# 32x32-block transposes on VectorE, with reordered expert weight rows, in place of three TensorE transposes per expert block

## The chip, the cores and the metric

The kernel runs on one core of one Trainium2 chip, in fp32. The metric is device time in microseconds (us), the median of several executions. In profiles PE is TensorE (PEld its weight loads), DVE is VectorE, ACT is ScalarE, POOL is GpSimd, and SP is SyncE, whose queue issues nearly all DMA transfers. PSUM is the tensor `ps`, eight banks of 128 x 512 fp32. TensorE's clock has two levels, 1.2 and 2.4 GHz; the profile gives the granted share of the higher one.

## The reference, cut to what matters

512 tokens of width 1024 go through two layers. Layer 0 mixes tokens by retention, layer 1 by a Conformer convolution. Each mixer is followed by a mixture of 32 experts in 4 groups, of which every token takes the best group and the best two experts inside it:

```python
h = rmsnorm(x, norm_ffn_g[i])
lg = xt @ w_rg + b_rg                       # group scores, top 1
le_sel = (xt @ w_re + b_re)[group]          # expert scores in the group, top 2
for each block of tokens that share an expert e:
    y = (silu(xblk @ w_gate[e]) * (xblk @ w_up[e])) @ w_down[e]
x = x + sum of the weighted y of each token
```

`w_gate[e]` and `w_up[e]` are 1024 x 512 and `w_down[e]` is 512 x 1024, all fp32: 6 MB for one expert, 192 MB for a layer. The kernel uses every expert in each layer.

## The kernel before, in words

The program is hand-scheduled: each engine runs its own list of instructions, and semaphores order them. The change lies in the expert stage, which occurs twice (layers `l` = 0 and 1).

**The weights.** An expert's weights come in three DMA transfers of 2 MB: `w_gu0` (gate and up, first half of the 1024 rows), `w_gu1` (second half) and `w_down`. There are nine places of 2 MB, three experts deep: `slots_of = [(0, 1, 2), (3, 4, 5), (6, 7, 8)]`. Places 0 to 5 lie in `ring`, 6 in `area_c`, 7 in `area_b` and 8 in `hT`; the profile names them so. The first three experts of a layer are loaded before its expert stage begins. SP then issues the three loads of expert e+3, in order, each once the last block of expert e has used the place: `gu_half` after the first half product, `gu_mm` after the second, `y_mm` after the down product (line 304 issues them). All go to one queue.

**The blocks.** An expert's tokens are cut into blocks of 32, at least one for each expert; the number is known only at run time, and loops with register bounds (`one_block`, `experts`) run over them. The profiled execution runs 46 blocks in layer 0 and 48 in layer 1. TensorE does for block t:

1. `gu` half 0 (L770): 16 products of the block's 32 rows, held transposed in `hgT`, with `w_gu0`, four column groups side by side.
2. `put_rows(0)` (L753): 16 products that scatter the block before, split in `y_hi` and `y_lo`, to the first 256 tokens by `slot_tok`, a 0/1 matrix. The result lies in banks 4 to 7.
3. `gu` half 1 (L770). Gate is then in `ps[:, 2, 0:128]` and up behind it, with 32 rows in each group of 32 partitions.
4. `pick_rows(t+1)` (L700): 16 products gather the next block's rows from `xn` by a 0/1 matrix, to `ps[:, 0, 0:256]`.
5. The transpose of `a_e`, the block's activation (L782).
6. `put_rows(1)` (L753): the other 256 tokens, again in banks 4 to 7. It waits until VectorE has added the first half to `x` (`added`).
7. `turn_block(t+1)` (L709): two transposes of `hg`, the next block's rows.
8. The down product `y` (L790) with `aT_e` and `w_down`.

VectorE adds the scattered tokens to `x` in four pieces (`add_tile`, L1132), computes `a_e` = silu(gate) * up (L1143), copies the picked rows from PSUM to `hg` (`stage`, L1020), multiplies their transpose by the norm gain into `hgT` (`turned_block`, L1008), forms `y_lo` (L1150), and prepares the next 0/1 matrix (`know_rows`, L996 to L1002). ScalarE computes `sg_e` = silu(gate) (L506), copies the transposed activation from PSUM to `aT_e` (L508) and rounds y to `y_hi` (L511). GpSimd builds `slot_tok` (L455).

A matrix row of `hg` holds, in partition 32g+s, columns 256g to 256g+255 of row s. TensorE's full 128 x 128 transposes bring column 256g+128c+p of that to partition p.

Of the kernel before, what the change touches and what calls it, by code (L numbers as in the profile page):

```python
# [21 lines left out]
ALU = mybir.AluOpType  # L22
# [7 lines left out]
P = 128  # L30
# [28 lines left out]
G_MIX, G_FFN, G_HEAD, B_PW1, B_DW, LN_G, LN_B, W_DW = 0, 16, 32, 48, 64, 72, 80, 88  # L59
NPAR = W_DW + KT * WIDTH  # L60

# [31 lines left out]
def program(nc, x_in, pos_in, const_in, decay_in, par_in, w_qk, w_v, w_g, w_out, w_pw1, w_pw2, b_pw2,  # L93
            w_router, b_router, w_gu0, w_gu1, w_down, g_final, tok_in, out):
    with ExitStack() as ctx:
        def sb(name, shape, dt=F32):
            return ctx.enter_context(nc.sbuf_tensor(name, shape, dt))
# [41 lines left out]
        block_rows = sb("block_rows", [P, NT, BLK])  # L139
        hg = sb("hg", [P, QW])  # L140
        hgT = sb("hgT", [P, KT, BLK])
# [116 lines left out]
        def both(name):  # L258
            return sems(name, NL)
# [6 lines left out]
        gu_half = both("gu_half")  # L266
        t1_mm, hgT_ready, gu_mm, silu_ready, act_ready, t2_mm, aT_ready, y_mm = (
            both(n) for n in ("t1_mm", "hgT_ready", "gu_mm", "silu_ready", "act_ready", "t2_mm", "aT_ready", "y_mm"))

# [190 lines left out]
        def _(act):  # L460
# [35 lines left out]
            def expert_blocks(l):  # L496
                act.wait_ge(exp_arg[l], 1)
                nc.scalar.activation(group_exp, group_exp, ACT.Exp).then_inc(exp_ready[l], 1)
                act.wait_ge(exp_arg[l], 2)
                nc.scalar.activation(expert_exp, expert_exp, ACT.Exp).then_inc(exp_ready[l], 1)  # L500
                act.wait_ge(cum_ready[l], 1)
                total = act.value_load(cum[0:1, NE:NE + 1], min_val=NE, max_val=NBLK - 1)
                act.wait_ge(idx_ready[l], 1)
                with act.Fori(0, total) as t:
                    act.wait_ge(gu_mm[l], t + 1)
                    nc.scalar.activation(sg_e[:, :], ps[:, 2, 0:P], ACT.Silu).then_inc(silu_ready[l], 1)  # L506
                    act.wait_ge(t2_mm[l], t + 1)
                    nc.scalar.copy(aT_e[:, :], ps[:, 3, 0:P]).then_inc(aT_ready[l], 1)  # L508
                    act.wait_ge(y_mm[l], t + 1)
                    act.wait_ge(second_mm[l], t + 1)  # L510
                    nc.scalar.activation(y_hi[:, :], ps[:, 3, P:P + QW], ACT.Copy,  # L511
                                         scale=slots[:, bass.ds(t + NBLK, 1)]).then_inc(y_rounded[l], 1)
# [117 lines left out]
        def _(pe):  # L630
# [73 lines left out]

            def turn_block(l, t):

                pe.wait_ge(staged[l], t + 1)
                for c in range(2):
                    last = nc.tensor.transpose(ps[:, 1, c * P:(c + 1) * P], hg[:, c * P:(c + 1) * P], ident)  # L709
                last.then_inc(t1_mm[l], 1)  # L710

            def route(l):
# [25 lines left out]
                pick_rows(l, 0)  # L738
                turn_block(l, 0)
                pe.wait_ge(spread_ready[l], 1)  # L740
# [17 lines left out]
            def one_block(l, t, turn, s_gu0, s_gu1, s_down):  # L758
# [21 lines left out]
                pick_rows(l, t + 1)  # L780
                pe.wait_ge(act_ready[l], t + 1)
                nc.tensor.transpose(ps[:, 3, 0:P], a_e[:, :], ident).then_inc(t2_mm[l], 1)  # L782
                pe.wait_ge(added[l], 4 * t + 6)
                put_rows(1, 4, second_mm[l])
                turn_block(l, t + 1)
                pe.wait_ge(aT_ready[l], t + 1)
# [154 lines left out]
        def _(dve):  # L941
# [61 lines left out]

            def turned_block(l, t, gain):

                dve.wait_ge(t1_mm[l], t + 1)
                for c in range(2):
                    ins = V.tensor_tensor(  # L1008
                        hgT[:, :, :].rearrange("p (q c) s -> p c q s", c=2)[:, c],
                        ps[:, 1, c * P:(c + 1) * P].rearrange("p (q s) -> p q s", q=4),  # L1010
                        par[:, gain:gain + KT].rearrange("p (q c) -> p c q", c=2)[:, c].unsqueeze(2)
                        .to_broadcast([P, 4, BLK]), ALU.mult)
                ins.then_inc(hgT_ready[l], 1)

            def stage(l, t):

                if not (isinstance(t, int) and t == 0):
                    dve.wait_ge(t1_mm[l], t)
                dve.wait_ge(pick_mm[l], t + 1)
                V.tensor_copy(hg[:, :], ps[:, 0, 0:QW]).then_inc(staged[l], 1)  # L1020

            def route(l, gain):
                dve.wait_ge(logitT_mm[l], 1)
# [18 lines left out]
                for i in range(NT):  # L1042
# [65 lines left out]
                                          coef[:, 0, :].unsqueeze(2).to_broadcast([P, 8, NBLK]), ALU.mult))  # L1108
                turned_block(l, 0, gain)
                link.done(V.tensor_tensor(block_hot_r[:, 1], block_hot[:, :, :],  # L1110
# [24 lines left out]

            def expert_blocks(l, gain, n):
                total = dve.value_load(cum[0:1, NE:NE + 1], min_val=NE, max_val=NBLK - 1)
                with dve.Fori(0, total) as t:
                    dve.wait_ge(first_mm[l], t + 1)
                    add_tile(0, 4).then_inc(added[l], 1)  # L1140
                    add_tile(1, 4).then_inc(added[l], 1)
                    dve.wait_ge(silu_ready[l], t + 1)
                    V.tensor_tensor(a_e[:, :], sg_e[:, :], ps[:, 2, P:2 * P], ALU.mult).then_inc(act_ready[l], 1)  # L1143
                    stage(l, t + 1)
                    dve.wait_ge(second_mm[l], t + 1)
                    add_tile(2, 4).then_inc(added[l], 1)
                    turned_block(l, t + 1, gain)
                    add_tile(3, 4).then_inc(added[l], 1)
# [96 lines left out]
            expert_norm(0, 1)  # L1245
            route(0, G_FFN)
            expert_blocks(0, G_FFN, 2)


# [85 lines left out]
            expert_norm(1, 3)  # L1335
            route(1, G_FFN + KT)
            expert_blocks(1, G_FFN + KT, 4)


# [83 lines left out]
```

## Time and profile before

| | us |
|---|---|
| median of 3 executions | 1647.12 (1646.97 to 1655.14) |
| the profiled execution, its own time | 1646.21 |
| span in its trace, first to last instruction | 1644.2 |
| expert loop of layer 0, first `gu` to the end of the last `y` | 473.0 to 922.2 |
| expert loop of layer 1 | 1165.8 to 1628.7 |

The span is cut into 40 slices of 41.1 us in the page's pictures, with a digit for the busy tenths of each. Chain rows, followed back from the last instruction, show what released what; a DMA row in the chain lasts from the issue of a transfer to its landing, with its time in the queue.

### The profile page before, as it was taken

How to read it: one execution, taken by the hardware profiler on the slowest of the kernel's cores; microseconds unless marked ns; L12 is line 12 of the kernel's file. 1: busy time of each engine (PE TensorE's matmuls, PEld its weight loads, DVE VectorE, ACT ScalarE, POOL GpSimd, SP SyncE). 2: the span in 40 equal slices, each digit the busy share in tenths (PEclk: the TensorE clock that was granted, in tenths of full speed). 3: DMA queues.
4: the chain of work that ended last, by engine and by line, in shares of the span. 5: the costliest groups of instructions: out<-in, count | busy, mean ns of one | idle time of the engine just before them, and what ended most of it. 6: DMA issues, size and time to landing. Idle time of an engine off the chain costs nothing.

```text
span 1644.2 us, 45941 instructions
## 1 busy us (share of the span) xinstructions
PE 1547.2 (94%) x19216; PEld 1008.3 (61%) x19217; DVE 967.9 (59%) x1669; ACT 467.8 (28%) x802; POOL 424.9 (26%) x371
## 2 busy tenths in 40 slices
PE   7999999999989999999889899889899999989996
PEld 6868678687645555555455588556555555555553
DVE  4222112220377777777657889943777777767777
ACT  5242422423312222222212432054122222222223
POOL 3434344243101121121112255511011121111211
PEclk9999999999999999999999999999999999999998
DMA  9212122122479999999999421036199999999994
GB/s 372 102 53 101 53 83 81 67 85 97 159 310 427 428 428 429 429 428 428 428 429 428 209 103 52 23 121 266 44 428 427 428 429 428 428 429 428 430 428 186
DMA packets 33849, 457.57 MB, mean 278 GB/s; under 512 B 3840, under 2 KB 3968, under 8 KB 6400
## 3 DMA queue, kind: packets, MB, share of 16 engines
q1 hardware_dynamic: 33648, 456.55, 66.5%
q8 instruction: 46, 0.75, 0.2%
q10 hardware_dynamic: 144, 0.17, 0.0%
q14 instruction: 11, 0.09, 0.0%
HBM read 454.61 MB, written 2.10 MB: 278 GB/s over the span
## 4 chain that ended last, share of the span: by engine, by line
PE 83%; DMA 8%; DVE 4%; issue 2%; ACT 2%; POOL 1%; DVEq 0%; SPq 0%; ACTq 0%; POOLq 0%
PE ps L770 19%; PE ps L658 10%; PE ps L660 10%; PE ps L659 10%; PE ps L790 9%; PE ps L700 9%; PE ps L753 7%; DMA area_b<-w_gu 6%; DMA ring<-w_down 2%; PE ps L858 2%; PE ps L709 2%; PE ps L782 1%; POOL area_c L439 1%; PE ps L908 1%; PE ps L850 1%
## 5 line engine op out<-in xcount | busy, mean ns | idle before, releaser
L1132 DVE TENSOR_TENSOR x<-x,ps 128x1024 f32<-128x1024 f32 x384 | 458.9, 1216 | 132.3 <-PE ps L753 132.3
L455 POOL TENSOR_SCALAR slot_tok<-trig,slot_now 128x512 fp32r<-128x512 f32 x94 | 147.0, 1564 | 719.3 <-PE ps L753 719.3
L424 POOL TENSOR_TENSOR w_lo<-ring,w_hi 128x512 fp32r<-128x512 f32 x176 | 237.8, 1354 | 356.1 <-ACT w_hi L474 356.0
L770 PE MATMUL ps<-ring,hgT 128*32 128x256 f32 x4160 | 255.9, 387 | 24.8 <-issue 21.0
L474 ACT CAST w_hi<-ring 128x512 fp32r<-128x512 f32 x176 | 108.8, 622 | 345.2 <-PE ps L660 345.2
L770 PEld LDWEIGHTS ps<-ring,hgT 128*32 128x32 f32 x4160 | 127.7, 111 | 122.0 <-issue 41.9
L700 PE MATMUL ps<-area_a,block_rows 128*32 128x256 f32 x3072 | 184.1, 380 | 2.6 <-DVE block_rows L1000 2.6
L700 PEld LDWEIGHTS ps<-area_a,block_rows 128*32 128x32 f32 x3072 | 100.4, 110 | 70.1 <-issue 5.3
L506 ACT ACT_TABLE_LOAD x94 | 120.6, 1283 | 33.2 <-DVEq L1122 31.5
L658 PE MATMUL ps<-w_hi,hT_hi 128*128 128x512 f32 x320 | 125.0, 391 | 2.9 <-DVE hT_lo L1322 2.9
L790 PE MATMUL ps<-ring,aT_e 128*32 128x256 f32 x2080 | 125.7, 382 | 0.2 <-DMA ring<-w_down 0.2
L659 PE MATMUL ps<-w_lo,hT_hi 128*128 128x512 f32 x320 | 124.6, 389 | 0.0
L660 PE MATMUL ps<-w_hi,hT_lo 128*128 128x512 f32 x320 | 124.5, 389 | 0.0
L753 PE MATMUL ps<-y_hi,slot_tok 32*128 32x256 f32 x1536 | 120.8, 329 | 2.8 <-DVE y_lo L1150 2.8
L511 ACT ACTIVATE y_hi<-ps,slots 128x256 fp32r<-128x256 f32 x94 | 44.6, 475 | 261.2 <-PE ps L790 261.2
L753 PEld LDWEIGHTS ps<-y_hi,slot_tok 32*128 32x128 f32 x1536 | 74.4, 184 | 55.3 <-issue 40.1
L506 ACT ACTIVATE sg_e<-ps 128x128 f32<-128x128 f32 x94 | 26.1, 278 | 274.1 <-PE ps L770 274.1
L658 PE MATMUL ps<-hT_hi,w_hi 128*128 128x512 f32 x256 | 99.8, 390 | 3.2 <-DVEq L1171 2.5
L753 PE MATMUL ps<-y_lo,slot_tok 32*128 32x256 f32 x1536 | 100.5, 276 | 0.0
L1020 DVE COPY hg<-ps 128x256 f32<-128x256 f32 x96 | 40.8, 425 | 100.4 <-PE ps L700 100.4
L659 PE MATMUL ps<-hT_lo,w_hi 128*128 128x512 f32 x256 | 99.6, 389 | 0.0
L660 PE MATMUL ps<-hT_hi,w_lo 128*128 128x512 f32 x256 | 99.6, 389 | 0.0
(217 smaller groups left out, 2067.4 us busy)
## 6 DMA issues: line engine op xcount, KB each, us to landing
ring<-w_gu SPq DMA_DIRECT2D x88, 2048.0 KB, 21.0
ring<-w_down SPq DMA_DIRECT2D x44, 2048.0 KB, 22.6
area_c<-w_gu SPq DMA_DIRECT2D x20, 2048.0 KB, 23.4
area_b<-w_gu SPq DMA_DIRECT2D x20, 2048.0 KB, 25.9
hT<-w_down SPq DMA_DIRECT2D x20, 2048.0 KB, 25.9
ring<-w_pw SPq DMA_DIRECT2D x6, 2048.0 KB, 11.1
ring<-w_qk SPq DMA_DIRECT2D x4, 2048.0 KB, 9.5
ring<-w_v SPq DMA_DIRECT2D x4, 2048.0 KB, 8.8
```

Source lines behind the costliest of these rows:

```text
L424: nc.gpsimd.tensor_tensor(w_lo[:, place, :], ring[:, s, at:at + 512], w_hi[:, place, :].bitcast(F32), ALU.subtract).then_inc(lo_ready, 1)
L455: nc.gpsimd.tensor_scalar(slot_tok[:, :], tok_number, slot_now[:, 0:1], None, ALU.is_equal).then_inc(tok_hot[l], 1)
L474: nc.scalar.copy(w_hi[:, place, :], ring[:, s, at:at + 512]).then_inc(hi_ready, 1)
L506: nc.scalar.activation(sg_e[:, :], ps[:, 2, 0:P], ACT.Silu).then_inc(silu_ready[l], 1)
L658: nc.tensor.matmul(at, lhs[0], rhs[0], start=start, stop=False)
L659: nc.tensor.matmul(at, lhs[0], rhs[1], start=False, stop=False)
L660: return nc.tensor.matmul(at, lhs[1], rhs[0], start=False, stop=stop)
L700: last = nc.tensor.matmul(ps[32 * g:32 * g + 32, 0, 0:QW], block_rows[:, i, :], xn[:, i, g * QW:(g + 1) * QW], start=(i == 0), stop=(i == ...
L753: last = nc.tensor.matmul(ps[:, bank + g, i * QW:(i + 1) * QW], slot_tok[rows, cols], part[rows, :], start=(i == 0 and n == 0), stop=(i == ...
L770: last = nc.tensor.matmul(ps[32 * g:32 * g + 32, 2, 0:256], hgT[:, n * (KT // 2) + k, :], gate_up[n][:, k, :, g * P:(g + 1) * P], start=(n ...
L790: last = nc.tensor.matmul(ps[32 * g:32 * g + 32, 3, P:P + QW], aT_e[:, k * BLK:(k + 1) * BLK], down[:, k, g * 256:(g + 1) * 256], start=(k ...
L1132: return V.tensor_tensor(x[:, i, :].rearrange("p (g c) -> p g c", g=4), x[:, i, :].rearrange("p (g c) -> p g c", g=4), ps[:, bank:bank + 4 ...
```

## The change

`hg` is made by VectorE's `transpose`, which transposes each 32 x 32 block by itself, straight from PSUM; `turned_block` then multiplies it by the gain, from SBUF to SBUF, in one instruction. `aT_e` is made by VectorE from `a_e` in the same way. TensorE's transposes of `hg` and `a_e` go, and so does ScalarE's copy to `aT_e`. After a blockwise transpose the partition 32g+j holds row 256g+32k+j of the model dimension in piece k, instead of row 128k+p. So the host lays the rows of all expert weights out in this order (`tiled`; the transfers have the same size and form), and the gains, 16 more columns of `par`, are laid out in it too (`strips`).

```diff
-        t1_mm, hgT_ready, gu_mm, silu_ready, act_ready, t2_mm, aT_ready, y_mm = (...)
+        hgT_ready, gu_mm, silu_ready, act_ready, aT_ready, y_mm = (...)
...
 # ScalarE, one block
                     nc.scalar.activation(sg_e[:, :], ps[:, 2, 0:P], ACT.Silu).then_inc(silu_ready[l], 1)
-                    act.wait_ge(t2_mm[l], t + 1)
-                    nc.scalar.copy(aT_e[:, :], ps[:, 3, 0:P]).then_inc(aT_ready[l], 1)
                     act.wait_ge(y_mm[l], t + 1)
...
 # TensorE
-            def turn_block(l, t):
-
-                pe.wait_ge(staged[l], t + 1)
-                for c in range(2):
-                    last = nc.tensor.transpose(ps[:, 1, c * P:(c + 1) * P], hg[:, c * P:(c + 1) * P], ident)
-                last.then_inc(t1_mm[l], 1)
...
                 pick_rows(l, t + 1)
-                pe.wait_ge(act_ready[l], t + 1)
-                nc.tensor.transpose(ps[:, 3, 0:P], a_e[:, :], ident).then_inc(t2_mm[l], 1)
                 pe.wait_ge(added[l], 4 * t + 6)
                 put_rows(1, 4, second_mm[l])
-                turn_block(l, t + 1)
                 pe.wait_ge(aT_ready[l], t + 1)
...
 # VectorE
             def stage(l, t):
 
                 if not (isinstance(t, int) and t == 0):
-                    dve.wait_ge(t1_mm[l], t)
+                    dve.wait_ge(hgT_ready[l], t)
                 dve.wait_ge(pick_mm[l], t + 1)
-                V.tensor_copy(hg[:, :], ps[:, 0, 0:QW]).then_inc(staged[l], 1)
+                V.transpose(hg[:, :, :].rearrange("p k s -> p (k s)"), ps[:, 0, 0:QW]).then_inc(staged[l], 1)
+
+            def turned_block(l, t):
+
+                dve.wait_ge(staged[l], t + 1)
+                V.tensor_tensor(hgT[:, :, :], hg[:, :, :],
+                                par[:, G_ROWS + KT * l:G_ROWS + KT * (l + 1)].unsqueeze(2).to_broadcast([P, KT, BLK]),
+                                ALU.mult).then_inc(hgT_ready[l], 1)
...
                     V.tensor_tensor(a_e[:, :], sg_e[:, :], ps[:, 2, P:2 * P], ALU.mult).then_inc(act_ready[l], 1)
+                    dve.wait_ge(act_ready[l], t + 1)
+                    V.transpose(aT_e[:, :], a_e[:, :]).then_inc(aT_ready[l], 1)
                     stage(l, t + 1)
+                    turned_block(l, t + 1)
                     dve.wait_ge(second_mm[l], t + 1)
                     add_tile(2, 4).then_inc(added[l], 1)
-                    turned_block(l, t + 1, gain)
                     add_tile(3, 4).then_inc(added[l], 1)
...
 # host
     def tiled(w):
 
         rows, cols = w.shape[2:]
-        return w.reshape(NL, NG, NPG, rows // P, P, cols).transpose(0, 2, 1, 4, 3, 5).reshape(NL, NE, P, SLOT)
+        return w.reshape(NL, NG, NPG, 4, rows // P, BLK, cols).transpose(0, 2, 1, 3, 5, 4, 6).reshape(NL, NE, P, SLOT)
```

The block of the loop as TensorE has it, from the second half product on. Before:

```order
L770 MATMUL ps<-ring,hgT 32x256 x16
L695 REGISTER_ALU
L700 MATMUL ps<-area_a,block_rows 32x256 x16
L782 MATMUL ps<-const,a_e 128x128
L783 REGISTER_ALU
L753 MATMUL ps<-y_hi,slot_tok 128x256 x4
L753 MATMUL ps<-y_lo,slot_tok 128x256 x4
L753 MATMUL ps<-y_hi,slot_tok 128x256 x4
L753 MATMUL ps<-y_lo,slot_tok 128x256 x4
L709 MATMUL ps<-const,hg 128x128 x2
L790 MATMUL ps<-ring,aT_e 32x256 x16
```

The same place on TensorE in the changed kernel:

```order
L761 MATMUL ps<-ring,hgT 32x256 x16
L694 REGISTER_ALU
L699 MATMUL ps<-area_a,block_rows 32x256 x16
L772 REGISTER_ALU
L744 MATMUL ps<-y_hi,slot_tok 128x256 x4
L744 MATMUL ps<-y_lo,slot_tok 128x256 x4
L744 MATMUL ps<-y_hi,slot_tok 128x256 x4
L744 MATMUL ps<-y_lo,slot_tok 128x256 x4
L778 MATMUL ps<-ring,aT_e 32x256 x16
```

The three transposes are gone, and nothing else on TensorE has moved. VectorE's block before, from its first two additions to `y_lo`:

```order
L1132 TENSOR_TENSOR x<-x,ps 128x1024 x2
L1143 TENSOR_TENSOR a_e<-sg_e,ps 128x128
L1019 REGISTER_ALU
L1020 COPY hg<-ps 128x256
L1132 TENSOR_TENSOR x<-x,ps 128x1024
L1008 TENSOR_TENSOR hgT<-ps,par 128x4x32 x2
L1132 TENSOR_TENSOR x<-x,ps 128x1024
L1150 ISA
L1150 SCALAR_TENSOR_TENSOR y_lo<-ps,slots,y_hi 128x256
```

The same place on VectorE in the changed kernel:

```order
L1116 TENSOR_TENSOR x<-x,ps 128x1024 x2
L1127 TENSOR_TENSOR a_e<-sg_e,ps 128x128
L1129 STREAM_TRANSPOSE aT_e<-a_e 128x128
L996 REGISTER_ALU
L997 STREAM_TRANSPOSE hg<-ps 128x256
L1002 TENSOR_TENSOR hgT<-hg,par 128x256
L1116 TENSOR_TENSOR x<-x,ps 128x1024 x2
L1136 ISA
L1136 SCALAR_TENSOR_TENSOR y_lo<-ps,slots,y_hi 128x256
```

The copy to `hg` has become a transpose, one more transpose stands ahead of it, and the multiplication into `hgT`, once in two parts between the last two additions, stands ahead of both.

## Rows read from the trace of the kernel before

**Rows 1.** The page's picture of the span, 40 slices: granted clock, DMA.
```profile
PEclk9999999999999999999999999999999999999998
DMA  9212122122479999999999421036199999999994
```

**Rows 2.** The page's DMA issues: form, count, KB, median us to landing.
```profile
ring<-w_gu SPq DMA_DIRECT2D x88, 2048.0 KB, 21.0
```

**Rows 3.** Windows of the expert stages: busy us by engine, PEclk, DMA share, GB/s.
```profile
790.00:840.00 50.00, 40.53 (x656) 22.42 (x648) 27.63 (x49) 9.21 (x16) 6.99 (x8) 0.93 1.01 428
1240.00:1290.00 50.00, 49.00 (x866) 28.29 (x862) 36.48 (x64) 11.78 (x21) 10.12 (x11) 1.00 1.01 429
1440.00:1490.00 50.00, 45.47 (x771) 26.07 (x767) 32.36 (x58) 11.23 (x19) 8.74 (x10) 0.97 1.01 429
```

**Rows 4.** The chain that ended last, one block: start us, us, what.
```profile
1572.22 1.75 PE ps L770 x32
1573.97 0.67 PE ps L753 x14
1574.64 1.86 PE ps L770 x32
1576.51 1.73 PE ps L700 x32
1578.23 0.26 PE ps L782
1578.49 0.68 PE ps L753 x15
1579.17 0.37 PE ps L709 x2
1579.54 1.86 PE ps L790 x32
```

**Rows 5.** The same chain: transfers in it, from issue to landing.
```profile
856.39 35.67 DMA ring<-w_down
...
1379.94 27.63 DMA area_b<-w_gu
...
1418.86 32.76 DMA area_b<-w_gu
```

**Rows 6.** SP's transfers: first expert loads of each layer's loop, and the last.
```profile
476.86 3.09 SPq L304 DMA_DIRECT2D ring<-w_gu  x2
...
1188.36 2.71 SPq L304 DMA_DIRECT2D ring<-w_gu  x2
...
1599.78 0.33 SPq L304 DMA_DIRECT2D ring<-w_down  x1
```

**Rows 7.** The chain again: the last down product of each layer.
```profile
920.30 1.91 PE ps L790 x32
...
1626.78 1.91 PE ps L790 x32
```

**Rows 8.** Timeline, VectorE and the down product in one block; idle before in brackets.
```profile
612.12 0.28 DVE L1143 TENSOR_TENSOR a_e<-sg_e,ps 128x128 f32<-128x128 f32 x1
613.45 0.42 DVE L1020 COPY hg<-ps 128x256 f32<-128x256 f32 x1 [1.05 <-PE ps L700]
...
614.37 1.22 DVE L1132 TENSOR_TENSOR x<-x,ps 128x1024 f32<-128x1024 f32 x1 [0.49 <-PE ps L753]
...
614.62 1.93 PE L790 MATMUL ps<-ring,aT_e 128*32 128x256 f32 x32
615.50 0.48 DVE L1008 TENSOR_TENSOR hgT<-ps,par 128x128 f32<-128x128 f32 x2
...
617.34 0.48 DVE L1150 SCALAR_TENSOR_TENSOR y_lo<-ps,slots,y_hi 128x256 fp32r<-128x256 f32 x1 [0.23 <-ACT y_hi L511]
```

**Rows 9.** The page's costliest groups: GpSimd's, busy, mean ns, idle before.
```profile
L455 POOL TENSOR_SCALAR slot_tok<-trig,slot_now 128x512 fp32r<-128x512 f32 x94 | 147.0, 1564 | 719.3 <-PE ps L753 719.3
```

**Rows 10.** Timeline, TensorE: a half product after a wait for its weights.
```profile
1446.78 3.60 PE L770 MATMUL ps<-area_c,hgT 128*32 128x256 f32 x32 [2.87 <-DMA area_c<-w_gu]
```

More of the change, by code:

```diff
@@ L59 @@
 G_MIX, G_FFN, G_HEAD, B_PW1, B_DW, LN_G, LN_B, W_DW = 0, 16, 32, 48, 64, 72, 80, 88
-NPAR = W_DW + KT * WIDTH
+G_ROWS = W_DW + KT * WIDTH
+NPAR = G_ROWS + NL * KT
 DEPTH = 3
@@ L139, in program @@
         block_rows = sb("block_rows", [P, NT, BLK])
-        hg = sb("hg", [P, QW])
+        hg = sb("hg", [P, KT, BLK])
         hgT = sb("hgT", [P, KT, BLK])
@@ L266, in program @@
         gu_half = both("gu_half")
-        t1_mm, hgT_ready, gu_mm, silu_ready, act_ready, t2_mm, aT_ready, y_mm = (
-            both(n) for n in ("t1_mm", "hgT_ready", "gu_mm", "silu_ready", "act_ready", "t2_mm", "aT_ready", "y_mm"))
+        hgT_ready, gu_mm, silu_ready, act_ready, aT_ready, y_mm = (
+            both(n) for n in ("hgT_ready", "gu_mm", "silu_ready", "act_ready", "aT_ready", "y_mm"))
         after_ret = [64, 64, 64, 64, 0, 0, 0, 0, 0]
@@ L738, in route @@
                 pick_rows(l, 0)
-                turn_block(l, 0)
                 pe.wait_ge(spread_ready[l], 1)
@@ L1002, in know_rows, with route @@
                 V.tensor_scalar(pos[:, :], pos[:, :], -float(BLK), None, ALU.add).then_inc(hot_step[l], 1)
[L1004 to L1013, printed above, removed]
             def stage(l, t):
                 if not (isinstance(t, int) and t == 0):
-                    dve.wait_ge(t1_mm[l], t)
+                    dve.wait_ge(hgT_ready[l], t)
                 dve.wait_ge(pick_mm[l], t + 1)
-                V.tensor_copy(hg[:, :], ps[:, 0, 0:QW]).then_inc(staged[l], 1)
-            def route(l, gain):
+                V.transpose(hg[:, :, :].rearrange("p k s -> p (k s)"), ps[:, 0, 0:QW]).then_inc(staged[l], 1)
[4 more added lines that the diff above has]
+                                ALU.mult).then_inc(hgT_ready[l], 1)
+            def route(l):
                 dve.wait_ge(logitT_mm[l], 1)
@@ L1108, in route @@
                                           coef[:, 0, :].unsqueeze(2).to_broadcast([P, 8, NBLK]), ALU.mult))
-                turned_block(l, 0, gain)
+                turned_block(l, 0)
                 link.done(V.tensor_tensor(block_hot_r[:, 1], block_hot[:, :, :],
@@ L1134, in add_tile, with expert_blocks @@
                                        ps[:, bank:bank + 4, i % 2 * QW:(i % 2 + 1) * QW], ALU.add)
-            def expert_blocks(l, gain, n):
+            def expert_blocks(l, n):
                 total = dve.value_load(cum[0:1, NE:NE + 1], min_val=NE, max_val=NBLK - 1)
@@ L1245, in _ @@
             expert_norm(0, 1)
-            route(0, G_FFN)
-            expert_blocks(0, G_FFN, 2)
+            route(0)
+            expert_blocks(0, 2)
             norm_lo(2, 1, G_MIX + KT)
@@ L1335, in _ @@
             expert_norm(1, 3)
-            route(1, G_FFN + KT)
-            expert_blocks(1, G_FFN + KT, 4)
+            route(1)
+            expert_blocks(1, 4)
 _NAMES = ("x_in", "pos_in", "const_in", "decay_in", "par_in", "w_qk", "w_v", "w_g", "w_out", "w_pw1", "w_pw2", "b_pw2",
@@ L1373, with strips @@
     const, decay = shape_constants()
+    def strips(w):
+        return w.reshape(NL, 4, KT, BLK).transpose(1, 3, 0, 2).reshape(P, NL * KT)
     def columns(w):
@@ L1385 @@
                           columns(a["conv_b_pw1"]), columns(crossed(a["conv_b_dw"])),
-                          columns(crossed(a["conv_ln_g"])), columns(crossed(a["conv_ln_b"])), taps], axis=1)
+                          columns(crossed(a["conv_ln_g"])), columns(crossed(a["conv_ln_b"])), taps,
+                          strips(a["norm_ffn_g"])], axis=1)
     w_in = a["ret_w_in"][0]
```

## The prediction, made before the changed kernel was run

> **What bounds the kernel now.** I began with the picture of the span. In its two long stretches where the DMA digit is 9, slices 12 to 22 and 29 to 39, the expert loops run [rows 1]. The windows there show both candidates for the bound at once: TensorE busy 49.0 of 50 us, and the DMA engines at a share of 1.01 with 428 GB/s [rows 3]. VectorE has 36.5 us of 50. So neither busy share decides; the question is which of the two is late at which point.
>
> The chain of waits answers it. Nearly all of it is TensorE, but at three places it passes through a transfer of 28 to 36 us [rows 5]. A transfer of 2 MB [rows 2] does not take so long: two landings in the same place `area_b`, at 1379.94 + 27.63 = 1407.57 and at 1418.86 + 32.76 = 1451.62, lie 44.05 us apart, and nine transfers (three experts) lie between them, so one takes 4.894 us, which is 2 MB at 428 GB/s. The rest of the 33 us is queue. The weights are a stream without gaps: 87 transfers in each layer, 426 us, from the release of the first place [rows 6] on. Where TensorE catches up with it, it waits: the windows from 790 and from 1440 us show 40.5 and 45.5 us busy of 50 instead of 49 [rows 3].
>
> So a faster block is worth nothing while the stream leads, and only what TensorE does after its last wait for weights can become shorter. Two such stretches exist.
>
> Layer 0: the last wait ends with the landing at 856.39 + 35.67 = 892.06 [rows 5]. Behind it stand the rest of that block and three whole blocks, up to the y at 920.30 [rows 7].
>
> Layer 1: the last wait ends at 1451.62 [rows 5]; from there to the y at 1626.78 [rows 7] TensorE runs 18 whole blocks. The last `w_down` is 34 transfers behind that landing: 1451.62 + 34 x 4.894 = 1618.0. Its y starts at 1626.78, so TensorE is 8.8 us behind the stream at the end. That lag is what the change can collect.
>
> **What a block loses.** One block of the chain is 1.75 + 0.67 + 1.86 + 1.73 + 0.26 + 0.68 + 0.37 + 1.86 = 9.18 us [rows 4]. The transpose of `a_e` (0.26) and the two of `hg` (0.37) go: 0.63 us. The neighbours that now meet (picked rows to `put_rows`, `put_rows` to y) meet elsewhere in the block already in the other order of the same shapes, the half product before `put_rows` at 1.75 and the one behind it at 1.86, so I add nothing for the seams.
>
> **What VectorE gains and loses.** It gets one more instruction of 128 elements, its copy from PSUM of 256 elements becomes a transpose, and the gain becomes one multiplication of 256 instead of two of 128 (0.48 together) [rows 8]. No transpose on VectorE is in the trace. From below I take the same shapes: 0.28 for 128 elements (`a_e`), 0.42 for the copy [rows 8]. From above I take the slowest rate of any row near it, GpSimd's 1.564 us for 512 elements [rows 9], 3.05 ns each: 0.39 and 0.78. I take the lower values, since a copy from the same bank by the same engine is the nearest row. The Trainium skill, VectorE: DVE Perf Modes, section The three transpose paths, gives 311 ns for a 128 x 128 bf16 transpose on VectorE; no run here shows it yet. With that price for `aT_e` and the same 30 ns more on `hg` the sum would come out the same, because both are covered as follows.
>
> `aT_e`: `a_e` ends at 612.40; VectorE then waited until 613.45 for the picked rows (1.05 idle) [rows 8]. The new transpose fits there even at 0.39 or 1.0 us. If that cover were gone, y would wait for it. `put_rows(1)`, which used to stand behind the transpose, now follows the picked rows at once; the additions that it waits for were done when `a_e` started, at 612.12, a microsecond earlier.
>
> `hg` and `hgT`: the transpose runs 613.45 to 613.87, the multiplication to about 614.3. The scatter now ends 0.26 earlier than the 614.37 at which the third addition started [rows 8], so the additions start at 614.3, bound by VectorE, and end near 616.65 without the multiplication between them. y starts at 613.99 instead of 614.62 [rows 8], `y_hi` follows, and `y_lo` may start 2.72 behind y as before, at 616.71. So VectorE has 0.06 us to spare there (it had 0.23 idle [rows 8]) and, after `know_rows`, about half a microsecond before the next additions. It is the engine that is late next. Of a costlier transpose of `hg`, between 0.1 and 0.5 us are free, and all beyond lengthens the block one for one.
>
> ScalarE loses a copy of 0.27 us, on which y depended; it only waits longer. 64 bytes more of `par` per partition and the new order of the weight rows change no transfer's size or form: 0. In front of each loop the first block's two transposes go, under VectorE's work on the block lists: 0.
>
> **The sum, with d = 0.63 saved in each block.** Layer 0: the landing at 892.06 stays, because the first place is released in the very first block [rows 6]. Three whole blocks behind it: 3d = 1.9 us. All other blocks of the layer (46 x 0.63 = 29 us in all) turn into waits for weights.
>
> Layer 1: the first place is released in its third block [rows 6], so the whole stream moves forward by 2d = 1.3 us. Without another wait the 18 blocks would give 18d + 2d = 12.6 us. But TensorE then catches the stream again. The tightest point is expert 28 (three blocks; experts 29 to 31 have one each, as the times of SP's transfers tell). Its `w_down` lies nine transfers before the last, 1618.0 - 44.0 = 1574.0, and is used at 1579.54 [rows 4]: 5.5 us of lag. Thirteen of the 18 blocks end there or before, and 13d = 8.2 is more, so TensorE waits. From there five blocks follow, up to the last y. So the gain is 5.5 + 2d + 5d = 9.9 us. With both layers it is the smaller of 23d and 5.5 + 10d, which cross at d = 0.42: 11.8 us here. Everything behind either loop keeps its length: the conv stage's own weights were already landed or queued, and the tail of layer 1 (additions, norm, output) has no transfer of weights in it.
>
> From this I take off a quarter of one slow half product in each layer, 2 x 0.25 x 1.67 = 0.8 us: after a wait for weights the clock can fall to its lower level, as in the half product of 3.60 us instead of 1.93 [rows 10], and the new waits, for the second halves of the gate and up weights of experts 30 and 28, stand right ahead of the two stretches. That leaves 11.0. The profiled execution took 1646.2 us, 0.9 under the median of the three runs; 1646.2 - 11.0 = 1635.2, and as a median 1636.1 us.
>
> **The rivals.**
>
> *The clock falls in the stretches that count* (0.10). For it: waits of 2 to 3 us are followed by a half product at 1.2 GHz in the trace [rows 10], and such waits become many. Against: most of what is slow then stands ahead of a landing and is hidden. Three slow half products behind the last waits cost 3 x 1.67 = 5.0: a gain of 6.8, 1640.3 us. The Trainium skill says the same of idle stretches (TensorE: Matmul & The Clock Gate, Part 1: activity releases the throttle, idleness lets it return); this trace agrees with its 3.60 us.
>
> *The transposes are slower than copies* (0.10). At 3.05 ns an element `hg` costs 0.36 more; d is then 0.38 to 0.63, the gain 8.7 to 11.8. At 1.0 us for `hg`, d is 0.15 to 0.5 and the gain 3.5 to 10.5: up to 1643 us.
>
> *VectorE becomes the bound and the kernel slower* (0.07). This needs the transpose of `hg` above 1.2 to 1.6 us. At four times the copy, 1.7, a block takes up to 0.5 us more than before, 94 x 0.5 = 47, less some 12 us that the waits for weights of today absorb (8.5 and 3.5 by rows 3): about 1680 us. Nothing in the trace has such a rate on VectorE; only that the instruction is unseen speaks for it.
>
> *Nothing comes of it, since the stream bounds the whole stage* (0.05). For it: the share of 1.01 everywhere. Against: the 8.8 us of lag at the end. It would leave 0 to 2 us: 1646 us.
>
> **Chances and range.** My own case has 0.68, with 1634 to 1638.5 us. A measurement tells about 0.5% (8.2 us) from no change; the gain passes that for d above 0.36. Faster by more than that: 0.68, and 0.05 from the first two rivals, 0.73. Within: 0.20. Slower: 0.07. The range, 1632.5 to 1642, takes in the clock's and the slower transpose's cases, and a gain of 14 if the lag before expert 28 is larger than reckoned.
>
> **What would show it.** In the trace after: blocks of 8.5 us where no weights are awaited; no TensorE row for the transposes; VectorE rows of about 0.3 and 0.43 us for its own; `y_lo` waiting for ScalarE by under 0.1 us or not at all; far more waits for `w_gu` in the middle of both loops; the last landing of layer 0 unchanged against the loop's start and that of layer 1 1.3 us nearer; loops shorter by 1.9 and 9.9 us. A block much over 8.6 us without a wait for weights refutes the VectorE part; a longer spacing than 4.89 us between landings refutes the stream part.

## The result, and the profile after

| | before | after |
|---|---|---|
| median, run side by side | 1647.36 us (6 runs) | 1636.38 us (6 runs, 1635.53 to 1638.92) |
| ratio, 95% interval | | 0.9927 (0.9913 to 0.9942) |
| span of the profiled execution | 1644.2 us | 1633.7 us |
| expert loop of layer 0, first `gu` to the start of the last `y` | 447.2 us | 446.1 us |
| expert loop of layer 1 | 460.9 us | 451.0 us |

The changed kernel is 11.0 us faster by the medians (12.0 by the ratio, 9.6 to 14.3 by its interval); the forecast was 1636.1 us. The picture of its span, from the page (granted clock, DMA), keeps its two stretches of nines in the DMA row. The granted clock has one more 8, in the middle, and its mean over the span is 0.976 instead of 0.986:

```profile
PEclk9999999999999999999899999999999999999998
DMA  9212112122379999999999620026299999999996
```

The same windows as [rows 3]: start and end, length, busy us of PE, PEld, DVE, ACT and POOL, then clock, DMA share and GB/s:

```profile
790.00:840.00 50.00, 37.21 (x596) 20.02 (x596) 27.22 (x45) 7.86 (x11) 6.99 (x8) 0.90 1.01 429
1240.00:1290.00 50.00, 49.00 (x916) 28.28 (x908) 41.05 (x69) 11.88 (x18) 10.47 (x12) 1.00 1.01 428
1440.00:1490.00 50.00, 44.67 (x804) 25.81 (x800) 35.20 (x60) 10.17 (x15) 7.94 (x10) 0.97 1.01 428
```

The DMA engines move what they moved before, 428 GB/s. TensorE, faster by a block's 0.63 us, waits more: 37.2 us busy in the first window instead of 40.5. VectorE's busy time rose from 36.5 to 41.1 us of 50 where no weights are awaited.

One block of the chain that ended last, against [rows 4]:

```profile
1582.51 1.73 PE ps L761 x32
1584.24 0.68 PE ps L744 x16
1584.91 1.86 PE ps L761 x32
1586.78 1.73 PE ps L699 x32
1588.51 0.67 PE ps L744 x15
1589.18 1.86 PE ps L778 x32
```

It sums to 8.53 us instead of 9.18. The rows of 0.26 (L782) and 0.37 (L709) are gone and the others have their old lengths within 0.02. VectorE and the down product in one block, from the timeline, against [rows 8] (idle before in brackets):

```profile
595.06 0.28 DVE L1127 TENSOR_TENSOR a_e<-sg_e,ps 128x128 f32<-128x128 f32 x1
595.37 0.31 DVE L1129 STREAM_TRANSPOSE aT_e<-a_e 128x128 f32<-128x128 f32 x1
596.40 0.45 DVE L997 STREAM_TRANSPOSE hg<-ps 128x256 f32<-128x256 f32 x1 [0.71 <-PE ps L699]
596.88 0.42 DVE L1002 TENSOR_TENSOR hgT<-hg,par 128x256 f32<-128x256 f32 x1
596.93 1.93 PE L778 MATMUL ps<-ring,aT_e 128*32 128x256 f32 x32
597.22 2.34 DVE L1116 TENSOR_TENSOR x<-x,ps 128x1024 f32<-128x1024 f32 x2
599.65 0.48 DVE L1136 SCALAR_TENSOR_TENSOR y_lo<-ps,slots,y_hi 128x256 fp32r<-128x256 f32 x1
```

The transposes take 0.31 and 0.45 us, against 0.42 for the copy that one of them replaces. `aT_e` runs in a hole that was 1.05 us wide and is 0.71 now. `y_lo` has no idle time before it in this block; in the view of waits it had one in all 94 blocks before (21.8 us in all) and has one in 9 now (6.6 us). The Trainium skill (VectorE: DVE Perf Modes, The three transpose paths) gives 311 ns for a 128 x 128 transpose in bf16 on VectorE; the one here is fp32 and took the same 0.31 us.

TensorE's waits for weights in the view of waits (total us, times, longest), for the changed kernel:

```profile
PE ps L761 <- DMA ring<-w_gu: 25.5, 16, 2.3
PE ps L761 <- DMA area_c<-w_gu: 12.0, 5, 2.9
PE ps L761 <- DMA area_b<-w_gu: 8.6, 5, 2.3
PE ps L778 <- DMA ring<-w_down: 3.9, 6, 0.7
PE ps L778 <- DMA hT<-w_down: 1.3, 2, 0.7
PE ps L761 <- issue: 16.4, 18, 1.1
```

For the kernel before, the same view:

```profile
PE ps L770 <- DMA area_c<-w_gu: 5.7, 2, 2.9
PE ps L770 <- DMA area_b<-w_gu: 3.8, 3, 2.3
PE ps L770 <- DMA ring<-w_gu: 3.7, 3, 2.5
PE ps L790 <- DMA ring<-w_down: 0.2, 1, 0.2
PE ps L770 <- issue: 21.0, 23, 1.9
```

The rows with a DMA hold 51.3 us instead of 13.4. So the account of the two loops reads: 94 x 0.63 = 59.2 us taken from TensorE's blocks, of which 37.9 came back as waits for weights. Another 12.0 came back as half products at the lower clock level behind such waits: in the timeline there are 12 of them (2.56 to 3.58 us, together 16.3 over 1.93) instead of 3 (4.3 over). 59.2 - 37.9 - 12.0 = 9.3 us are left, and the two loops are 11.0 us shorter (1.1 and 9.9). The rest consists of smaller terms of both signs, read from the gaps and starts of TensorE's instructions inside the loops. The "issue" gaps ahead of half products, in which TensorE waits for nothing that the profile shows, are 4.4 us shorter (probably since some are now part of a wait for weights). Layer 1's first half product takes 2.75 us instead of 3.64. Against them, the other products, mostly those right behind slow half products, take 3.7 us more. 9.3 + 4.4 + 0.9 - 3.7 = 10.9.

The last wait in each loop, with what follows it, in the chain of the changed kernel (DMA rows last from issue to landing), against [rows 5, 10]:

```profile
850.03 36.74 DMA ring<-w_gu
886.77 0.04 issue
886.81 3.53 PE ps L761 x32
...
1539.15 26.90 DMA ring<-w_gu
1566.05 0.04 issue
1566.09 3.55 PE ps L761 x32
...
1572.11 1.86 PE ps L778 x32
```

Layer 0's last wait still lies three whole blocks ahead of the end, layer 1's moved from 18 blocks ahead to expert 28, five blocks ahead. Both are followed by a half product of 3.5 us, the lower clock level.

SP's first transfers of the loops, against [rows 6]:

```profile
476.68 3.16 SPq L305 DMA_DIRECT2D ring<-w_gu  x2
...
1185.21 2.71 SPq L305 DMA_DIRECT2D ring<-w_gu  x2
```

Layer 1's first place is released 20.04 us into its loop, which starts at 1165.17; before, it was 22.59.

Two single rows answer to [rows 2, 7]. In the page's DMA issues the transfers take 27.9 us to land instead of 21.0: TensorE frees the places sooner, and the queue ahead of them is longer. In the group of the last down product (one tile, one window: count, shortest, median and longest ns, first and last start) layer 1's begins at 1616.2. Its weights landed at 1614.94, 1.26 us earlier; before, they had lain there for 8.7 us.

```profile
ring<-w_gu SPq DMA_DIRECT2D x88, 2048.0 KB, 27.9
```

```profile
L778 PE MATMUL ps<-ring,aT_e x32: 378/379/404, 1616.2 to 1617.8; 128*32 128x256 f32 x32
```

### The profile page after: what moved, and what is told of

It reads as the page before. It is cut to its first block, busy times and chain, and to the rows that moved or that the text cites. A ratio compares the mean times of both kernels' runs of the same rounds, so it can differ in the third digit from the quotient of the medians.

```text
span 1633.7 us, 45273 instructions
## 1 busy us (share of the span) xinstructions
PE 1502.6 (92%) x18930; PEld 982.6 (60%) x18931; DVE 994.7 (61%) x1667; ACT 442.5 (27%) x708; POOL 424.3 (26%) x371
## 4 chain that ended last, share of the span: by engine, by line
PE 67%; DMA 19%; DVE 10%; ACT 2%; issue 1%; POOL 0%; DVEq 0%; SPq 0%; ACTq 0%
PE ps L761 16%; PE ps L657 9%; PE ps L658 9%; PE ps L659 8%; PE ps L778 8%; PE ps L699 7%; DMA area_b<-w_gu 7%; DMA ring<-w_gu 6%; PE ps L744 5%; DMA hT<-w_down 4%; DVE area_c L1278 4%; PE ps L846 2%; DVE ring L1278 2%; DMA ring<-w_down 2%; PE ps L838 1%
## 5 line engine op out<-in xcount | busy, mean ns | idle before, releaser
L1116 DVE TENSOR_TENSOR x<-x,ps 128x1024 f32<-128x1024 f32 x384 | 450.8, 1215 | 100.3 <-PE ps L744 100.3
L761 PE MATMUL ps<-ring,hgT 128*32 128x256 f32 x4160 | 263.2, 396 | 42.1 <-DMA ring<-w_gu 25.5
L778 PEld LDWEIGHTS ps<-ring,aT_e 128*32 128x32 f32 x2080 | 62.3, 109 | 45.4 <-issue 5.2
## 6 DMA issues: line engine op xcount, KB each, us to landing
ring<-w_gu SPq DMA_DIRECT2D x88, 2048.0 KB, 27.9
```

Of the source, the lines that this page charges most:

```text
L761: last = nc.tensor.matmul(ps[32 * g:32 * g + 32, 2, 0:256], hgT[:, n * (KT // 2) + k, :], gate_up[n][:, k, :, g * P:(g + 1) * P], start=(n ...
L778: last = nc.tensor.matmul(ps[32 * g:32 * g + 32, 3, P:P + QW], aT_e[:, k * BLK:(k + 1) * BLK], down[:, k, g * 256:(g + 1) * 256], start=(k ...
L1116: return V.tensor_tensor(x[:, i, :].rearrange("p (g c) -> p g c", g=4), x[:, i, :].rearrange("p (g c) -> p g c", g=4), ps[:, bank:bank + 4 ...
```

## The experiments

Two theories stand against each other throughout. The **stream theory** is the prediction's: the weights' stream sets the pace, and only the blocks behind the last wait for it can shorten a layer. The **proportional rival**: each block is 0.63 us shorter, and a fixed share of it reaches the end everywhere, so that the parts add up. Below, "lag" is the time from the last landing of weights in layer 1 to the start of the `y` that uses them. Each loop and each lag is read from the trace of one execution. Outside the loops executions differ too: the stretch between the loops took 245.5, 246.1 and 250.6 us in three profiled executions (of the kernel before, and of two variants of it below that differ from it only later, in layer 1). So a difference of a few us between two totals says little by itself, and the loops say more.

**Half of the change: block rows only.** `hg` goes by VectorE, `a_e` still by TensorE and ScalarE, and `w_down` keeps its old order of rows. Of the diff above only the lines of `stage`, `turned_block`, `turn_block` and `strips` are made.

```diff
-                turn_block(l, t + 1)
-                V.tensor_copy(hg[:, :], ps[:, 0, 0:QW]).then_inc(staged[l], 1)
+                V.transpose(hg[:, :, :].rearrange("p k s -> p (k s)"), ps[:, 0, 0:QW]).then_inc(staged[l], 1)
```

> Only the block rows are transposed by VectorE; the activation goes through TensorE and ScalarE as before, with w_down in its old row order. d is 0.37 us a block. Theory of the lag (only what TensorE does after its last waits for weights counts; gain the smaller of 23d and 5.5 + 10d): 8.5 us faster than before, up to 1.2 us less for each slow half product right ahead of the last stretches. Rival, every block's saving counts in the same proportion as in the whole change (11.0 us for 0.63): 6.4 us. Rival, VectorE's work has no room: block over 8.85 us.

Measured: 1641.67 us beside 1648.97 for before, ratio 0.9957 (0.9941 to 0.9974), 7.3 us by the medians and 7.1 by the ratio. The block is 8.82 us, 0.37 less, as expected, so VectorE had the room. The time lies between the 8.5 us of the stream theory and the 6.4 of its rival, and by itself decides nothing. Layer 1's loop is 452.8 us and its lag 2.1.

**The other half: activation only.**

```diff
-                    act.wait_ge(t2_mm[l], t + 1)
-                    nc.scalar.copy(aT_e[:, :], ps[:, 3, 0:P]).then_inc(aT_ready[l], 1)
-                pe.wait_ge(act_ready[l], t + 1)
-                nc.tensor.transpose(ps[:, 3, 0:P], a_e[:, :], ident).then_inc(t2_mm[l], 1)
+                    dve.wait_ge(act_ready[l], t + 1)
+                    V.transpose(aT_e[:, :], a_e[:, :]).then_inc(aT_ready[l], 1)
```

> Only the activation is transposed by VectorE, with w_down in the new row order; the block rows go through TensorE as before. d is 0.26 us. Theory of the lag: 6.0 us faster than before, and the gains of this run and of the one with the rows only add up to more (14.5) than the whole change gave (11.0), because alone neither makes TensorE catch the stream again before the last five blocks of layer 1. Rival, gain in proportion to the saving: 4.5 us, and the two add up to 11.0.

Measured: 1642.37 us, ratio 0.996 (0.9946 to 0.9974), so 6.6 us. The block is 8.93, the loop of layer 1 455.9 us, the lag 5.6. By the ratios the two halves sum to 7.1 + 6.6 = 13.7 us, and the whole is worth 12.0 (11.0 by the medians), which leans to the stream theory. The interval of each half is 2.7 us to either side, so this sum alone does not decide. Both halves also had a faster first half product than the changed kernel: in layer 0 it took 2.59 and 2.51 us instead of 3.64, and the last weights landed 432.6 and 432.8 us into the loop, instead of 433.9, which flatters each of them by about 1.2 us. What speaks clearly is the lag of layer 1, 8.7, then 5.6, 2.1 and 1.3 us: it is used up.

**VectorE's room: one transpose more.** The changed kernel with the transpose of `hg` done twice.

```diff
+                for spare in spares:
+                    V.transpose(spare[:, :], ps[:, 0, 0:QW])
```

> The changed kernel with the transpose of the block rows issued once more to a spare tile: VectorE has 0.42 to 0.45 us more in each block, ahead of its last two additions. If VectorE has about 0.4 us of room (by the gap between its y_lo and the next scatter), the block stays within 0.1 us of 8.53 and the time within 1 us of the change's, 10 to 11 us faster than before. If it has only the 0.06 us of the prediction, the block is 8.9 us and the gain 5 to 6 us.

Measured: 1638.65 us, ratio 0.9943 (0.9923 to 0.9964), 10.3 us faster than before by the medians; the block is 8.55, as in the changed kernel (its median there, 8.53 to 8.60). The additional transpose starts 0.37 us before the next one, so it takes 0.37 us of VectorE's time, and the block has room for all of it.

**Three transposes more.** As above, with three places to write to, two of them in `trig`.

> The changed kernel with three more transposes of the block rows to spare tiles, 1.3 us more on VectorE in each block. Theory: room of 0.4, the rest one for one: block 8.53 + 0.95 = 9.5 us, 0.3 us over the kernel before, hence slower than before by about 14 us (the waits for weights of before absorb a part of 94 x 0.3 = 28 us). Rival, VectorE has room for all of it (its busy share is 0.8): no slower than the change. Rival, it had no room at all: block 9.8 us, 30 us slower than before.

Measured: 1643.69 us, ratio 0.9967 (0.9952 to 0.9982). This was expected to lose 14 us to before and gained 5.4: the expectation failed. The timeline shows two reasons.

```profile
595.04 0.45 DVE L1000 STREAM_TRANSPOSE spare<-ps 128x256 f32<-128x256 f32 x1 [0.71 <-PE ps L700]
595.41 0.74 DVE L1000 STREAM_TRANSPOSE trig<-ps 128x256 f32<-128x256 f32 x2
596.07 0.41 DVE L1001 STREAM_TRANSPOSE hg<-ps 128x256 f32<-128x256 f32 x1
596.51 0.43 DVE L1006 TENSOR_TENSOR hgT<-hg,par 128x256 f32<-128x256 f32 x1
596.86 2.35 DVE L1120 TENSOR_TENSOR x<-x,ps 128x1024 f32<-128x1024 f32 x2
...
599.73 0.39 PE L745 MATMUL ps<-y_hi,slot_tok 32*128 32x256 f32 x4 [0.50 <-DVE y_lo L1140]
```

From the first transpose to the additions it takes 1.82 us, against 0.82 in the changed kernel: three transposes add 1.00, not three times 0.45, since each starts before the one ahead of it has ended. And the block is 9.09 us, 0.54 more than 8.55; the last row shows what it waits for, the `y_lo` of the block before. If the block grows one for one past the room, as the prediction has it ("between 0.1 and 0.5 us are free, and all beyond lengthens the block one for one"), VectorE had 1.00 - 0.54 = 0.46 us to spare. The run before this one fits (0.37 cost nothing); the slope itself was not measured, since only this run lies past the room. At 9.09 a block is still shorter than the 9.18 of before, and 19 of the 92 took 8.55 to 8.67 even here, those of layer 1 each right behind a block with a change of expert or a wait for weights. The lag of layer 1 is 3.8 us.

**Half of the stream.** In layer 1 the loads behind the first nine bring only the first half of each place, so that half of the expert weights of 29 experts is left out (old values stand in their stead). This was done to the kernel before and to the changed one. Nothing else differs.

```diff
+                n = SLOT // 2 if l == 1 else SLOT
+                sp.dma_start(places[s][:, 0:n], w[:, 0:n]).then_inc(slot_loaded[s], 16)
```

On the kernel before:

> The kernel before, but in layer 1 every weight load after the first nine moves only the first half of its place (the other half keeps old weights), so the stream of layer 1 needs half the time and TensorE never waits for it. Theory of the lag: TensorE's own pace is left, about 7 us faster than before (the waits for weights in layer 1 go). Rival, TensorE sets the time of the whole stage already: no change.

On the changed kernel:

> The same halved stream in layer 1 under the changed kernel. Theory of the lag: now all 48 blocks of layer 1 count in full, 48 x 0.63 = 30.2 us, and with layer 0's 1 to 2 us this run is 31 to 32 us faster than the one before it with the same halved stream, where the change with the full stream gives 10 to 12. Rival, the 11 us are all that the shorter block is worth: 10 to 12 us here as well.

Measured: 1638.56 us (ratio 0.9931, 0.9907 to 0.9954) and 1606.85 us (0.9733, 0.97 to 0.9767). Both are about as the stream theory had them: 8.9 us faster than before where about 7 were expected, and 31.7 apart where 31 to 32 were. The change is worth 31.7 us once layer 1 moves half the bytes, and 11 when it moves all. Layer 1's loops are 452.3 and 423.7 us; the difference of 28.6 is 48 blocks of 0.60. Windows of the first of the two, then of the second, with the columns of [rows 3]:

```profile
1440.00:1490.00 50.00, 49.05 (x875) 28.46 (x871) 37.03 (x63) 11.78 (x21) 8.73 (x10) 1.00 0.57 204
```

```profile
1440.00:1490.00 50.00, 48.01 (x900) 27.73 (x892) 41.15 (x69) 11.81 (x18) 10.50 (x12) 1.00 0.63 224
```

With the DMA share at 0.57 and 0.63, TensorE is 48 to 49 us busy of 50 in both; VectorE, with one more instruction in a shorter block, reaches 41 us and still holds nothing up. This is the whole value of the change on TensorE. The pair refutes the rival of a fixed share, and VectorE as a bound.

**One transfer more.** An additional 2 MB is moved in layer 1, ahead of the last six loads of weights, to a buffer that nobody reads. If the end hangs on the stream, this costs a transfer's time; where TensorE is late by more than it, nothing.

```diff
+                    if l == 1 and e == LOOPED:
+                        sp.dma_start(aside[:, :], w_gu0[l, e]).then_inc(out_stored, 16)
```

On the kernel before:

> The kernel before with one more transfer of 2 MB (to a buffer in HBM that nobody reads) in the queue ahead of the last six weight loads of layer 1: the last landings come 4.9 us later, or up to twice that as it reads and writes HBM. Theory of the lag: TensorE is 8.7 us behind the last landing, so at 4.9 us the time does not change (0 to 1 us). Rival, the stream sets the time in layer 1: 4.9 us slower.

On the changed kernel:

> The changed kernel with the same additional transfer. Theory of the lag: only 1.3 us of lag are left, so 4.9 us of stream cost 3.6 us and more, against the changed kernel without it (that is 7 to 8.5 us faster than the kernel before instead of 10 to 12). Rival, as much lag as before is left: no cost.

Measured: 1647.55 us (ratio 1.0008, 0.9989 to 1.0028), no cost by the medians, though the interval reaches a cost of 4.6 us; and 1641.61 us (0.997, 0.9952 to 0.9987). That is 5.8 us faster than before by the medians, where 7 to 8.5 were expected, and 5.2 us more than the changed kernel, which was run at another time (7 by the ratios). The traces are clearer. In the kernel before, the lag of 8.7 went down to 4.3 us and the loop stayed at 461.0. In the changed one, the last landing moved by 5.5 us and not 4.9, and the loop by 4.3 us; the lag took the rest. What the totals show beyond 4.3 us, 1 to 3 us, is not explained. The chain of the changed kernel with the transfer ends in a wait:

```profile
1592.29 29.45 DMA ring<-w_down
1621.74 0.14 issue
1621.87 1.97 PE ps L781 x32
```

The last `y` of the program starts 0.13 us after its weights land. In the kernel before, the lag absorbed the transfer; in the changed one nothing does.

**The start of the stream.** With both layers on the stream, its start should count. It hangs on the first half product of a loop, which in the changed kernel stands behind 3.79 us of idle time of TensorE and one short product, and in layer 0 takes 3.64 us instead of 1.93, the lower clock. From the timeline of the changed kernel (the second row is the first half product of layer 0):

```profile
470.66 2.04 PE L733 MATMUL ps<-block_hot_r,slot_hot_r 128*128 128x216 f32 x8 [3.79 <-DVE block_hot_r L1096]
472.84 3.64 PE L761 MATMUL ps<-ring,hgT 128*32 128x256 f32 x32
```

The first attempt put eight idle products there (products of constants whose result nobody reads, to keep TensorE busy), with

```diff
                 pick_rows(l, 0)
+                stay_awake(4, 8)
```

> The changed kernel with eight idle products (128 x 512, 0.46 us each in the trace of the changed kernel) on TensorE behind the first gather of each layer, where it now sits idle for 3.79 us ahead of the product at 470.66 and 1163.24; nothing else differs. In the changed kernel the first half product then takes 3.64 us in layer 0 and 2.75 us in layer 1, instead of 1.93. Theory (the stream of weights sets the end of both layers, and it starts when the first half product releases the first place): the first release comes earlier by 1.7 us in layer 0 and 0.8 us in layer 1, the last landings move by as much, and the kernel becomes 2.5 us faster than the changed one, about 1633.9 us; up to 4 if the product at 470.66 also gets shorter. Rival 1 (the start of the stream decides nothing, the end is set by TensorE's blocks): the two half products save their 2.5 us only if TensorE never waits afterwards, and since it waits in the middle of both loops nothing is left: 1636.4 us. Rival 2 (the clock of the first block doesn't follow from the idle time ahead of it): the first half products stay at 3.6 and 2.8 us, no change, or slower by up to 0.5 us in each layer if the idle products end after the releaser.

Measured: 1639.14 us beside 1649.06 for before, ratio 0.9931 (0.9913 to 0.995): no gain over the changed kernel's 0.9927, where 2.5 us were expected. The half products took 1.93 us and the loops were 444.2 and 449.4 us, shorter by 1.8 and 1.6 than the changed kernel's; but the products took 7.13 us and not 3.7, since one is two rows of the profile, and the loops started 1.9 us later after the gather. The loops became shorter as the theory had it; the filler was mis-sized.

So four products, and the changed kernel once more beside it:

> As the run with eight idle products, but with four. Their time was mis-read there: a row of x8 in the profile is four products (two passes each), so eight took 7.13 us, not 3.7, and ran past the 3.79 us of idle time; the way from the first gather to the loop grew from 6.0 to 7.9 us in each layer, while both loops became shorter (by 1.8 and 1.6 us). Four take 3.68 us and fit. Theory (the stream's start, set by the first release, moves the end of each layer): the loops are as short as with eight (444.2 and 449.4 us, against 446.1 and 451.0 in the changed kernel), and the way to them is 0.4 to 0.6 us shorter than in the changed kernel instead of 1.9 longer; together 4 to 4.5 us faster than the changed kernel run beside it. Rival (the loops were shorter by chance of the clock in their middle): no more than 1 us faster than the changed kernel.

> The changed kernel once more, unchanged, on the chip of the run with four idle products, so that the two are compared there. Both theories: a ratio of 0.9927 to the kernel before, as measured first (0.9913 to 0.9942).

Measured: 1633.31 us (6 runs, 1630.95 to 1638.0), ratio 0.9915 (0.9898 to 0.9932), and 1637.97 us for the changed kernel (6 runs, 1632.28 to 1638.51), ratio 0.9931 (0.9914 to 0.9948). That is 4.7 us between the medians, where 4 to 4.5 were expected and the rival had at most 1. It is not clear of the noise: by the ratios it is 2.6 us, and both the intervals and the ranges overlap. The profile of the kernel with four:

```profile
466.97 3.70 PE L653 MATMUL ps<-const 128*128 128x512 f32 x8
470.83 1.15 PE L734 MATMUL ps<-block_hot_r,slot_hot_r 128*128 128x216 f32 x8 [0.17 <-DVE block_hot_r L1097]
473.00 1.93 PE L762 MATMUL ps<-ring,hgT 128*32 128x256 f32 x32 [1.02 <-issue]
```

The way from the gather to the loop did not get shorter, as I had expected it to (5.97 us in both): what the product at 470.83 gains, an "issue" gap of 1.02 takes. The loops did: 443.5 and 449.2 us, against 446.4 and 451.0 in the changed kernel run beside it, and that is 4.65 us, in one execution of each. The first half products account for 3.64 - 1.93 = 1.7 and 2.68 - 1.93 = 0.8 us of it. Another 1.8 us come from the two slow half products ahead of the stretches that count, which stood in both profiles of the changed kernel and are not there now: in its second one the `y` behind them started 0.97 and 1.07 us after its weights had landed, and now 0.13 in both layers. The chain passes through waits for `w_down` at those places:

```profile
851.84 38.35 DMA ring<-w_down
...
1540.03 27.22 DMA ring<-w_down
1567.25 0.14 issue
1567.38 1.93 PE ps L779 x32
```

The waits ahead of those two half products, from the timelines: 2.10 and 1.99 us in the changed kernel, 2.11 and 2.00 in its second run, all four followed by 3.5 to 3.6 us; 1.13 and 1.69 us with four idle products, both followed by 1.93. With eight, 2.12 us (3.57 behind it) and 1.11 us (1.93). So an earlier stream seems to help a second time, by shortening the waits at which the clock falls. That it does is an inference from these eight waits in four executions, and the 2.12 with eight idle products stands against it; the first effect, the release, is shown by the first half products themselves.

## Why the prediction was right

**What bounds the kernel.** Right, and shown. If TensorE's or VectorE's time alone set the end, the change would be worth as much with the full stream as with half of it; it is worth 11 us and 31.7. If the stream alone set it, one transfer more would cost both kernels about the same; layer 1's loop grew by 0.1 us in the kernel before and by 4.3 in the changed one. It takes both, with the lag between them, as the prediction has it.

**The block.** Forecast 9.18 - 0.63 = 8.55, measured 8.53 to 8.60 where no weights are awaited. The seams cost nothing, as assumed.

**VectorE.** Transposes of 0.28 to 0.39 and 0.42 to 0.78 us were bounded and the lower ends taken; they are 0.31 and 0.45. The slip is the room in the pipeline: 0.06 us at `y_lo` was reckoned as the next thing to be late, with "between 0.1 and 0.5" free in all. One transpose more (0.37) costs nothing and three more show 0.46, near the upper end. `y_lo` may be late by several tenths without any cost, because TensorE needs it only behind the next block's first half product. In the block shown above `y_lo` ends at 600.13, and the scatter that uses it starts at 600.55, 0.42 us later. With three more transposes the same scatter starts 0.13 us after `y_lo` (599.60 to 599.73), so 0.29 of the 0.42 was free. The other 0.18 lies ahead of `y_lo`: in the changed kernel it starts 0.09 us behind the end of the additions, where it is still held by `y_hi` (which ends at 599.51), and with three more 0.09 ahead of their end. 0.29 + 0.18 is the room of 0.46 that the block's length shows.

**Layer 0.** Forecast 1.9, measured 1.1 us. The mechanism (three whole blocks behind the last landing) stands in the chain. In the trace the `w_down` of expert 30 lands at 892.04, which is 419.2 us into the loop and 0.2 later than before. Before, `y` began 0.13 us after this landing; now it began 0.72 after it, because of the slow half product. 1.9 - 0.2 - 0.6 = 1.1.

**Layer 1.** Forecast 9.9, measured 9.9, and this is partly luck. The tightest point was expert 28, as forecast. But the first release came 2.55 us earlier in the loop (20.04 instead of 22.59) and not 2d = 1.26: by chance the first block of this loop ran 1.3 us faster than in the profiled execution of before, 0.9 of it in its first half product (2.75 us instead of 3.64; in other executions of the two kernels it took 2.54 to 3.64 us). Against it, the slow half product at 1566.09 made `y` start at 1572.04 instead of 1570.94, where its weights landed, 1.1 us. 5.5 + 1.26 + 1.3 + 5 x 0.63 - 1.1 = 10.1.

**The clock.** The prediction named the two places where a slow half product would hurt, and took off a quarter of one for each, 0.8 us. Both were there, in the profile of the changed kernel and again in its second one. Over the 0.13 us that `y` takes after a landing at the least, they cost 0.6 and 1.0 us (0.8 and 0.9 in the second): the term was too small by 0.8 us. The 1.3 at layer 1's start, of which the prediction had nothing, outweighed it, so the sum came right with errors of opposite sign. The Trainium skill (TensorE: Matmul & The Clock Gate, Part 1) has idle stretches bring the throttle back; the 3.53 and 3.55 us, behind waits of 2.10 and 1.99 us, agree in direction. The filled gap, after which the first half product takes 1.93 instead of 3.64, is the other half of that rule.

**The rest.** Between the loops 0.7 us were lost (246.25 instead of 245.54), of which the prediction had nothing; it lies in the conv stage, which the change does not touch, and is small beside the 5 us by which that stretch differs between executions of the same code. 0.2 + 1.1 - 0.7 + 9.9 is the 10.5 us of the two spans.

## What to carry to other kernels

Where an engine and a stream are both nearly full, find the last wait for the stream: an edit is worth its saving times the blocks behind that wait, until the lag is used up, and not times all blocks. After such an edit, look for the next gain in the stream: the instruction that releases its first buffer, and the clock at which it runs. Test the reading by moving the stream rather than the engine (halve it, or add one transfer), which here gave 31.7 us against 11, and a loop longer by 4.3 us against 0.1, where the parts of the edit differed from the rival by one or two.

## What the runs showed of the hardware

- VectorE's transposes by 32 x 32 blocks cost little more than other instructions of their shape: 0.31 us for 128 x 128 in fp32 (the multiplication to `a_e`: 0.28) and 0.45 for 128 x 256 from PSUM (copy: 0.42). Four in a row start 0.33 to 0.37 us apart, so the row's duration overstates what one more costs.
- Waits of a few us on TensorE had a price of their own. In the profile of the changed kernel, of 12 waits of 0.47 to 1.90 us for gate and up weights one was followed by a half product slower than 1.93 us, of 14 waits of 1.99 to 2.88 us eleven were (2.56 to 3.58). With eight idle products ahead of the loops, of 15 waits of 2.12 to 2.96 us eight were. The same wait of 2.87 us had 1.93 behind it at 735.08 and 3.43 at 1443.70, so the wait alone does not decide it.
- The first half product of layer 0 starts 2.17 to 2.21 us after the start of the product ahead of it in 12 of the 13 profiles, whatever that product takes: 2.04 us with an idle 0.13 behind it in the changed kernel, 1.40 and 0.80 in the kernel before with one transfer more, 1.15 and 1.02 with four idle products. A faster product there gains nothing; an "issue" gap takes its place. Only with eight idle products, where the product itself starts late, is it 1.38 us.
